# Query and key transposes, the last gate and its head sums, and the memory keys' norm moved among the attention's steps; other PSUM banks for the output projection

## What is computed

```python
u_hy, q, k, v = jnp.split(h @ w_in[i], split_at, axis=-1)
y_hy = hyena_mixer(u_hy, ...)      # per order: z = gate * (fft_long_conv(z, k_f) + skip * z)
y_at = gqa_mixer(q, k, v, ...)     # q, k: norm per head, rope; 8 q heads, 2 kv heads, 64 wide
y = jnp.concatenate([group_rms_norm(y_hy, out_norm_hyena[i], HYENA_GROUPS),
                     group_rms_norm(y_at, out_norm_attn[i], N_Q_HEADS)], axis=-1)
x = x + y @ w_out[i]
x = x + memory_cross_attn(rms_norm(x, ...), rms_norm(mem, ...), ...)   # its keys k are normed per head
x = x + hier_moe(...)
```

## Time and profile before

| | us |
|---|---|
| median of 3 runs | 842.38 |
| the three runs | 845.26, 835.30, 842.38 |
| the profiled execution: its time | 835.02 |
| its span in the profile | 833.2 |
| PE busy in the span | 767.9 (92%) |
| DVE busy | 605.9 (73%) |
| ACT busy | 457.6 (55%) |
| mean granted clock of PE | 0.958 |

### The profile page before, as it was taken

One profiled execution on the slowest core, in us unless ns is written; L12 is line 12 of the kernel. 1 busy time (PEld: TensorE's weight loads), 2 busy tenths in 40 slices (PEclk: granted clock), 3 DMA queues, 4 the chain that ended last, 5 costly groups with the idle time before them and its releaser, 6 DMA issues.

```text
span 833.2 us, 10882 instructions
## 1 busy us (share of the span) xinstructions
PE 767.9 (92%) x3722; PEld 624.0 (75%) x3722; DVE 605.9 (73%) x921; ACT 457.6 (55%) x672; POOL 73.6 (9%) x86
## 2 busy tenths in 40 slices
PE   5799999988988999999895898999999999999994
PEld 3564858776877899978774587778888888888883
DVE  5468383996899578624538357879999989999882
ACT  6653233121234766622357243468888788888772
POOL 0000000000000000000000000102232223232111
PEclk8899999999999799989999799899999999999997
DMA  8720203020120200012221187599999999999941
GB/s 287 272 84 19 77 25 101 26 76 1 51 76 26 101 1 2 1 40 88 76 77 50 39 325 274 213 369 356 376 372 370 373 379 384 372 377 372 336 170 20
DMA packets 28542, 146.53 MB, mean 176 GB/s; under 512 B 4791, under 2 KB 6711, under 8 KB 21976
## 3 DMA queue, kind: packets, MB, share of 16 engines
q1 hardware_dynamic: 23320, 135.53, 43.7%
q0 software_dynamic: 5184, 10.50, 4.8%
HBM read 141.81 MB, written 12.58 MB: 185 GB/s over the span
## 4 chain that ended last, share of the span: by engine, by line
PE 75%; DVE 13%; ACT 5%; DMA 3%; issue 2%; SPq 1%; POOL 0%; DVEq 0%; POOLq 0%; ACTq 0%
PE bank L1817 16%; PE bank L1762 15%; PE bank L2141 11%; PE bank L2143 11%; PE bank L2142 10%; PE bank L1769 4%; PE bank L1829 2%; PE bank L2136 2%; DMA x_in<-in_x 1%; DMA w_raw<-in_w_in 1%; PE bank L2053 1%; DVE w_lo L1051 1%; PE bank L2055 1%; PE bank L2054 1%; ACT junk L628 1%
## 5 line engine op out<-in xcount | busy, mean ns | idle before, releaser
L1688 DVE TENSOR_TENSOR e_lo<-slot,e_hi 128x1024 fp32r<-128x1024 f32 x192 | 221.5, 1219 | 9.7 <-ACT e_hi L937 9.5
L937 ACT ACTIVATE e_hi<-slot 128x1024 fp32r<-128x1024 f32 x192 | 188.6, 1061 | 9.7 <-PE bank L2143 6.6
L1051 DVE TENSOR_TENSOR w_lo<-w_raw,w_hi 128x1024 fp32r<-128x1024 f32 x41 | 49.6, 1223 | 77.5 <-ACT w_hi L667 77.3
L2141 PE MATMUL bank<-e_hi,hgT_hi 128*128 128x512 f32 x256 | 102.0, 399 | 1.4 <-DVE hgT_lo L1706 1.2
L667 ACT ACTIVATE w_hi<-w_raw 128x1024 fp32r<-128x1024 f32 x41 | 42.8, 1062 | 108.5 <-DMA w_raw<-in_w_in 63.6
L2143 PE MATMUL bank<-e_hi,hgT_lo 128*128 128x512 f32 x256 | 100.7, 393 | 0.0
L2142 PE MATMUL bank<-e_lo,hgT_hi 128*128 128x512 f32 x256 | 100.3, 392 | 0.0
L2141 PEld LDWEIGHTS bank<-e_hi,hgT_hi 128*128 128x128 f32 x256 | 48.7, 190 | 11.6 <-DVE hgT_lo L1706 1.4
L2143 PEld LDWEIGHTS bank<-e_hi,hgT_lo 128*128 128x128 f32 x256 | 48.4, 189 | 10.4
L2142 PEld LDWEIGHTS bank<-e_lo,hgT_hi 128*128 128x128 f32 x256 | 48.6, 190 | 9.7
L2141 PE MATMUL bank<-e_hi,gaT_hi 128*128 128x512 f32 x120 | 48.1, 401 | 0.0
(11 more groups left out here) (370 smaller groups left out, 1698.1 us busy)
## 6 DMA issues: line engine op xcount, KB each, us to landing
slot<-in_w_down SPq DMA_DIRECT2D x16, 2048.0 KB, 15.9
slot<-in_w_gate SPq DMA_DIRECT2D x16, 2048.0 KB, 14.6
slot<-in_w_up SPq DMA_DIRECT2D x16, 2048.0 KB, 15.7
w_raw<-in_w_in SPq DMA_DIRECT2D x18, 512.0 KB, 3.6
w_raw<-in_w_out SPq DMA_DIRECT2D x8, 512.0 KB, 3.7
w_raw<-in_w_k_mem SPq DMA_DIRECT2D x4, 512.0 KB, 6.3
x_in<-in_x SPq DMA_DIRECT2D x4, 512.0 KB, 9.2
w_raw<-in_w_v_mem SPq DMA_DIRECT2D x4, 512.0 KB, 5.3
```

The lines of the kernel that those rows point to most:

```text
L937: act.activation(e_hi[buffer(b, j)][:], slot[slot_][:, 1024 * part:1024 * (part + 1)], ACT.Copy).then_inc(s_ehi, 1)
L1051: dve.tensor_tensor(w_lo[slot_][:], w_raw[slot_][:], w_hi[slot_][:].bitcast(F32), ALU.subtract)\
L1688: dve.tensor_tensor(e_lo[slot_][:, at_], slot[slot_][:, at_], e_hi[buffer(b, j)][:].bitcast(F32), ALU.subtract)\
L2141: pe.matmul(dst, act_hi, w_hi_, start=first, stop=False)
```

## The change

- Ahead of the attention PE transposes only the keys of the first kv head (`kT` 0 and 1) and the queries of heads 0 to 2. Head 3's queries are transposed in step -2, `kT` 2 and 3 and head 4's queries in step -1, heads 5, 6 and 7 in steps 0, 1 and 2, each between `PT` and `pv` of its step. ACT evacuates each right behind. A score waits only for its own head's banks.
- The gate of order 2 is cut in two: the part that reads the banks (`skipped`) stays ahead of the attention, the rest (`gated(1, c)`) goes to DVE's steps 2 to 5, the squares to ACT's steps 3 to 6, `hn` to PE's step 7, its square root to ACT's step 8, the inverse to DVE's step 9. `HR_STEPS` move from 5, 8, 11, 14 to 14, 17, 20, 23.
- `v_lo` is written by DVE behind the second maximum, and no longer ahead of the gate.
- The memory keys' norm (a reciprocal and four products on DVE) moves from the stretch before the rope to steps 12 and 13; `weight_hi(28)` and `weight_lo(28)` go to steps 15 and 16; the `mkT` transposes go to PE behind `wo1`, their evacuation on ACT behind `weight_hi(35, 2)`.
- Two single-element activations call for a function's table ahead of use: Exp ahead of the first key bank, Sqrt behind the last step.
- The banks of the first half of `wo0` are those of 0 to 5 that come next in turn, and `yT` takes 6, 7 and the next two.

```diff
+GATED_STEP = 2
+HN_STEP = GATED_STEP + CT + 1
+MK_STEP = 12
-HR_STEP = 5
+HR_STEP = 14
...
+            elif j[0] == "yT":
+                number[j] = len(number)
+                b = (6, 7, after[4], after[5])[j[1]]
+            elif j[:2] == ("wout", 0):
+                number[j] = len(number)
+                b = after[j[2]]
+                turn = b + 1
...
+            if n == last_s:
+                after = [(turn + c) % 6 for c in range(6)]
...
+            act.activation(small[:, 398:399], eps, ACT.Exp)
+            kT_evac(0)
+            kT_evac(1)
+            for h in range(3):
+                qT_evac(h)
...
             for s in range(AHEAD):
                 gqa_exp(s)
+            qT_evac(3)
             for s in range(NSEQ):
                 gqa_pt_hi(s)
                 if s + AHEAD < NSEQ:
                     gqa_exp(s + AHEAD)
+                if s == 0:
+                    kT_evac(2)
+                    kT_evac(3)
+                if s + 4 < NQ:
+                    qT_evac(s + 4)
+                if GATED_STEP < s <= GATED_STEP + CT:
+                    y_square(s - GATED_STEP - 1)
+                if s == HN_STEP + 1:
+                    hyena_root()
+                if s == MK_STEP + 3:
+                    weight_hi(28, 1)
                 if s % NQ == 3 and s > NQ:
                     out_square(s // NQ - 1)
+            act.activation(small[:, 398:399], eps, ACT.Sqrt)
...
                 gqa_lo(s)
-                if s == 2:
+                if GATED_STEP <= s < GATED_STEP + CT:
+                    gated(1, s - GATED_STEP)
+                if s == HN_STEP + 2:
                     hyena_inverse()
+                if MK_STEP <= s < MK_STEP + MT:
+                    mk_normed(s - MK_STEP)
+                if s == MK_STEP + 4:
+                    weight_lo(28, 1)
...
-                if s == 0:
-                    for p in range(NQ):
-                        wait_freed(pe, ("qT", p))
-                    for j in range(2 * NKV):
-                        wait_freed(pe, ("kT", j))
+                if s < NQ:
+                    wait_freed(pe, ("qT", h))
+                if s in (0, NQ // 2):
+                    for part in range(2):
+                        wait_freed(pe, ("kT", 2 * (h // 4) + part))
```

More of the change, by code:

```diff
@@ L81, in psum_jobs @@
         jobs += [("inv", o, c) for c in range(CT)]
-    jobs += [("mkT", j) for j in range(2)]
-    jobs += [("qT", h) for h in range(NQ)] + [("kT", j) for j in range(2 * NKV)] + [("hn",)]
+    jobs += [("kT", 0), ("kT", 1), ("qT", 0), ("qT", 1), ("qT", 2)]
     n = TT * NQ
@@ L92, in psum_jobs @@
             jobs += [("PT", s + 2)]
+        if s == -1:
+            jobs += [("kT", 2), ("kT", 3)]
+        if s + 5 < NQ:
+            jobs += [("qT", s + 5)]
+        if s == HN_STEP:
+            jobs += [("hn",)]
         if s in HR_STEPS:
@@ L96, in psum_jobs @@
     jobs += [("wout", h, i) for h in range(2) for i in range(TT)]
+    jobs += [("mkT", j) for j in range(2)]
     jobs += [("hT", 1, k) for k in range(KT)]
@@ L799, in _, with kT_evac, qT_evac, y_square @@
             q_split_hi(3, 5)
[L800 to L805, removed]
+            def kT_evac(j):
+                wait_filled(act, ("kT", j))
+                free(act.activation(kT[:, j // 2, j % 2, :], bank(("kT", j))[:], ACT.Copy), ("kT", j))
+            def qT_evac(h):
+                wait_filled(act, ("qT", h))
+                free(act.activation(qT[:, h, :], bank(("qT", h))[:], ACT.Copy), ("qT", h))
+            def y_square(c):
                 act.wait_ge(s_z, CT + c + 1)
                 act.activation(y_sq[:, c, :], u[:, c, :], ACT.Square).then_inc(s_ysq, 1)
[L808 to L817 removed]
+            def hyena_root():
+                job = ("hn",)
+                wait_filled(act, job)
+                free(act.activation(small[:, 280:312], bank(job)[:, 0:32], ACT.Sqrt, bias=eps, scale=1.0 / HD), job)
+            act.activation(small[:, 398:399], eps, ACT.Exp)
[3 more added lines that the diff above has]
+                qT_evac(h)
             def gqa_exp(s):
@@ L864, in _ @@
             weight_hi(35, 2)
+            for j in range(2):
+                wait_filled(act, ("mkT", j))
+                free(act.activation(mkT[:, 2 * j:2 * j + 2, :].rearrange("p h m -> p (h m)"), bank(("mkT", j))[:], ACT.Copy),
+                     ("mkT", j))
             for k in range(KT):
@@ L1224, in pointwise, with skipped, gated @@
                 ins.then_inc(s_ab, 1)
[L1226 to L1236, removed]
+            def skipped(o, c):
+                job = ("inv", o, c)
+                wait_filled(dve, job)
+                n = CT * o + c
+                free(dve.scalar_tensor_tensor(u[:, c, :], u[:, c, :], small[:, 72 + n:73 + n], bank(job)[:],
+                                              ALU.mult, ALU.add), job)
+            def gated(o, c):
+                n = CT * o + c
+                wait_freed(dve, ("inv", o, c))
+                dve.scalar_tensor_tensor(u[:, c, :], u[:, c, :], small[:, 60 + n:61 + n], u[:, CT * (o + 1) + c, :],
+                                         ALU.mult, ALU.mult).then_inc(s_z, 1)
             def qk(i):
@@ L1262, in _ @@
             outer_taps(8)
-            gated(0)
+            for c in range(CT):
+                skipped(0, c)
+                gated(0, c)
             z_lo(1)
@@ L2003, in _ @@
             chunk_jobs("wo1", yT_hi, yT_lo)
+            pe.wait_ge(s_mkn, MT)
+            for j in range(2):
+                transposes(("mkT", j), [mk[:, m, h * MHD:(h + 1) * MHD] for h in (2 * j, 2 * j + 1) for m in range(MT)])
             hT_jobs(1, x2, residual_done("wout"))
```

59 lines of the change are left out of this document (33 added, 26 removed).

## The result

The changed kernel is **slower by 1%**: a median of 847.06 us over 20 runs (839.47 to 884.99) beside 836.86 us for the kernel before (20 runs, 833.98 to 896.28), with a ratio of 1.0098 (95% interval 1.0074 to 1.0122). The forecast was 3.1 us faster. The table of runs that stood ahead of it had three runs and a median of 842.38; the twenty put the kernel before at 836.86, so on them the forecast reads 833.8, and its range 827.0 to 841.0; the result lies outside the range either way.

What follows compares the result with a forecast made beforehand. PE's own work bounds the kernel, so gains must come from its waits or lower clock; nine terms summed to -3.1 us, 831.9 for the profiled execution and 839.3 for the median, range over all cases 832.5 to 846.5.

Steps and rivals of the forecast that it cites:

- Term 1: Start of the scores: fewer transposes ahead bring PT(0) to 271.4 in place of 282.73, -11.3 us.
- Term 2: PT(0) to score 5: five added transpose banks and two waits on evacuations, clock rising mid-stretch, +3.2 us (+1.0 to +6.6).
- Terms 3 and 4: Queries 6 and 7 transposed in steps 1 and 2, +0.7 us; hn moved into step 7, +3.5 us.
- Term 5: ACT at step 8: root and two table loads delay the next exponential without making PE wait, 0 us, 1.1 in reserve.
- Term 6: Behind hn in step 7: the clock falls to half for 3 to 7 us, +1.7 us (0 to +3.4).
- A: Rival: half clock lasts to score 5 and the fall behind hn lasts as before; +2.0 us, 844.4, chance 0.2.
- Term 7: DVE's added work in steps 2 to 5, 12, 13, 16 and 19 fits its reserve: 0 us, at worst +1.0.
- Term 8: Output projection: PE's wait for ACT to read pv's last bank goes, -1.3 us.
- Term 9: Memory keys behind wo1: their evacuation delays ACT's first hT_hi and DVE's rest, +0.4 us (0 to +1.0).
- C: Rival: transposes don't lift the clock from 266 to score 5; +0.3 us, 842.7, chance 0.06.
- D: Rival: ACT's strict order makes PE wait 0.9 us in each of ten steps; +5.9 us, 848.3, chance 0.1.
- B: Rival: the clock holds up to score 5 (1.4 us) and behind hn (0); -6.6 us, 835.8, chance 0.17.

Runs made afterwards that it cites:

- e8: Changed kernel with 32 unread dense products of 448 columns, two ahead of each of the sixteen narrow head-sum products: 836.45 us, ratio 0.999 to the kernel before.
- e7: Kernel before with thirty-two unread two-column matmuls, shaped like the head sums, added in attention step 7: 888.58 us, ratio 1.0614.
- e13: Changed kernel with dense head sums but the old banks for yT and the projection's first half: 828.18 us, ratio 0.9901 to the kernel before.
- e6: Changed kernel with the head sums left out, one product of 32 columns in their place: 832.79 us, ratio 0.9931 to the kernel before.
- e10: Kernel before with only the new banks for yT and the output projection's first half: 836.76 us, ratio 0.9985.
- e3: Changed kernel with Hyena's norm three steps later (HR_STEP 17 for 14): 855.28 us, ratio 1.0216 to the kernel before.
- e11: Changed kernel with gates, squares and sums back ahead of score 0, nine transposes left among the steps: 839.1 us, ratio 1.0017 to the kernel before.
- e1: Changed kernel with the sixteen head-sum products dealt out four at a time over steps 4 to 7: median 884.18 us.
- e2: Changed kernel with eight unread dense products of 448 columns among the head sums in step 7: 848.98 us, ratio 1.0151 to the kernel before.
- e4: Changed kernel with Hyena's norm three steps earlier (HR_STEP 11 for 14): median 877.42 us.
- e9: Changed kernel with head sums as four dense 512-column products, turned back by four small transposes a step later: 830.69 us, ratio 0.9919 to the kernel before.

## Why the prediction was wrong, point by point

The forecast's sum was -3.1 us on the profiled execution; that came out as +8.95.

- *Term 1, start of the scores* (-11.3): -11.1. Right, by the steps given.
- *Term 2, `PT(0)` to score 5* (+3.2): 8.61 us for 6.18, +2.4. The two waits on ACT's `qT` are there (0.78 and 0.84, said 0.65 to 0.8), with one of 0.59 for an exponential that wasn't named. The clock was full all the way, for which the working had 7.2 us, so the clock was priced 2.2 too dear and the rest 1.4 too cheap; that the sum came near is partly luck. A bank of queries costs 0.44 us at the full clock in the steps, and not 0.36.
- *Terms 3 and 4* (+0.7, +3.5): `hn` took 3.5 us, and steps 1 and 2 took 2.68 us each (score 5 at 280.25, 6 at 282.93, 7 at 285.61) for 2.24, so +0.9. What is left of the loss from score 5 to the projection is 17.3 + 1.3 (the wait that went) - 3.5 - 0.9 = 14.2; the last `pv` products ran 0.9 us at the lower level for 1.8 before, which saved 0.5, so the half clock behind `hn` cost 14.2 + 0.5 = 14.7.
- *Term 5, ACT at step 8* (0): right. PE waited for nothing between 299 and 367; those steps are slow ones, but e8 has the same loads at the full clock and no wait near them. ACT's timeline in after, where the second load starts once PE has its next `pT_hi`:

```profile
299.24 0.29 ACT L834 ACTIVATE small<-bank,small 128x32 f32<-128x32 f32 x1 [3.05 <-PE bank L2006]
...
300.04 1.28 ACT L847 ACT_TABLE_LOAD   x1
301.33 0.78 ACT L847 ACTIVATE pr<-bank,small 128x512 f32<-128x512 f32 x1
```

  The exponential starts at 301.33, right at the load's end (300.04 + 1.28). The Trainium skill (ScalarE: Activation LUTs, "What ACT_TABLE_LOAD costs") has a load of the same length and as much again for a drain, 2.7 us in all; no such drain shows here.
- ***Term 6, the clock after `hn`* (+1.7, at most +3.4): this step failed.** It measured 14.6 by the steps' pitch, 14.7 by what the other terms leave. Without this term the forecast was -4.8, and the measured change without it is 8.95 - 14.6 = -5.7. That there would be a fall right behind `hn` was right. Its length was taken from two stretches of the kernel before: one of 3.8 us, which ended among products of 512 columns in the projection, and one of 6.8, which had waits in it and ended in the first `pv`, behind two scores and three banks of transposes with no `pv` between them. Neither was the work that follows here, steps of two products of 512 columns, four transposes and twelve products of 64, and e7 shows what that work can do with a clock that is down: nothing, for 105 us. How long the stretch lasts then differs between executions, so that 14.6 is the price in this one. The earlier trace rows showed the steps *keep* a full clock; that they could also *restore* one was assumed from it, and does not follow. That gap was not priced in any rival either: A's top for this term was the same 3.4. None of the three signs that the prediction named as proof against it came either (score 0 after 272, waits in each of steps 0 to 8, over 2 us behind the attention); of what it expected of the profile, the "3 to 7 us" at 0.5 is what failed, with 30.72.
- *Term 7, DVE's load* (0, at worst +1.0): no wait in after, but steps 12 and 13 ran there at 4.27 us each, and DVE reached the load of step 16 as the slow stretch ended. Where the clock stays up, a late maximum does reach PE: e13 waits 0.53 us at 313.77 behind the memory keys' norm, and at the load of step 16 (the weight's rest and Hyena's norm) e6 waits 0.84 at 319.50 and e8 0.71 at 328.68. The slow stretch hid this term; at the full clock it costs near its "at worst".
- *Term 8, the projection's banks* (-1.3): the wait went, in after and in e10. What it is worth in the end isn't shown (e10: 0.9985, 0.9952 to 1.0019; e13 doesn't have the old wait).
- *Term 9, memory keys* (+0.4): from the first product of the projection to the first of `wq` 54.40 for 54.49, of which the shorter half-clock stretch there (2.6 us for 3.8) saved 0.6: +0.5. The evacuation came between `w_hi` and the first `hT_hi` as said (420.03, then 420.98); that PE waits 0.86 us for it ahead of its last transposes was not named, and at `hT_lo` it waits 0.80 for the 1.23 of before.

*Rivals.* C fell. The clock stayed full through the twenty transposes from 266.53, which stand without a gap, and it came back in or right behind runs of them in after, e3, e11 and e13. The rule behind C (the Trainium skill, TensorE: Matmul & The Clock Gate, "PE-mode transpose"), that transposes don't count as busy the same way, isn't borne out here, though e1, e2, e4, e7 and e9 show that eight in a row aren't always enough. D fell: the waits after `PT(0)` are 2.2 us in all, and there are none from step 1 on. B was right on the clock in term 2, though its 1.4 us was 2.4, and wrong for term 6. The forecast's error was not in any of these, and its range, whose top was A, did not hold the result.

## What to carry to other kernels

Price a move of PE work by what surrounds it at its new place. Work with hardly a column in it (here two per product) costs its own time while PE waits anyway. In the middle of steps that are mostly 64-column products it cost 18 us in after (its own 3.6 and the 14.6 of the slow stretch) and 51 in e7, since these steps by themselves did not bring back the level that it lost. Before counting a fall of the clock at the length of one seen elsewhere, look at which instructions ended that one. If such work must lie in the steps, change its shape so that the long side moves: here that turned +1% into -1% at the same place. And when a slower stretch hides an engine's load, check that load again in a run without the slow stretch, as e6, e8 and e13 do here for DVE.

## What the runs showed of the hardware that was not expected

- A PE that was busy did not bring back a full clock: in e1, e2 and e4 it had the 0.50 level without a gap for 105.8 (e4) to 109.2 us (e1, e2), nearly all of it the attention's steps, and the level rose 3 to 6 us into the projection, whose products are all of 512 columns. At 1.00 the same kind of steps ran for 54.6 us (e6), 54.7 (e8) and 75.1 (e11).
- 3.6 us of two-column products cost 51 us (e7). With 8 dense products among them the clock still fell, with 32 it did not (e2, e8).
- The same place of the program (315.6) loses the clock in two executions, for 3.4 us in one and for 78.5 in the other (e13, e9). What decides that stays open, and so does why eight transposes in a row brought it back in after, e3 and e13 and not in e1, e2, e4, e7 and e9.
